# A decoder layer on one core: an earlier end of the output gate, key scaling in the own sum, scores in the key two, and the mix work of the last head spread out

## What is computed

```python
proj = rmsnorm(x) @ w_in                      # 4096 -> q, k, v, o, z of each head, and the rest
q, k = split(silu(causal_conv([m_q, m_k], w_conv)))
s = (q @ k.T) * exp(decay)                    # scores of one head, 256 x 256, causal
num, qn = s @ v, s.sum(-1)                    # "numerator" and its row sums
h = num / max(abs(qn), exp(-m))
h = rmsnorm(sigmoid(m_o) * h) * gain * silu(m_z)   # output gate o, gate z
out = rmsnorm(x + concat([h, attention * silu(a_z)]) @ w_out)
```

## Time and profile before

| | |
|---|---|
| median of 3 runs | 1752.15 us (1752.09 to 1752.25) |
| profiled execution, its own time | 1752.96 us |
| its span, first to last instruction | 1751.2 us |
| PE busy, matmuls | 1733.5 us, 8000 |
| DVE, ACT busy | 1313.6 us, 947.6 us |
| weight transfers (w_raw) | 614 of 512 KB, 202 GB/s over the span |
| heads' twos in the trace | 798 to 1401 us |

### The profile page before, as it was taken

The page is one execution under the profiler, slowest core; times in us unless marked ns, Lnnn a source line. Parts: engine busy times, 40 slices in busy tenths (PEclk is TensorE's granted clock), DMA queues, the critical chain, the costliest instruction groups (busy, mean ns, idle before and its releaser), DMA issues.

```text
span 1751.2 us, 23455 instructions
## 1 busy us (share of the span) xinstructions
PE 1733.5 (99%) x8000; PEld 1437.0 (82%) x8000; DVE 1313.6 (75%) x1679; ACT 947.6 (54%) x1318; POOL 20.0 (1%) x33
## 2 busy tenths in 40 slices
PE   9999999999999999999999999999999999999997
PEld 7888888888888888888888888888888788888886
DVE  7556786566675756668887888788878988888876
ACT  7535555455555555545555555555555665564553
POOL 0000000000000000000000000000000000000000
PEclk9999999999999999999999999999999999999999
DMA  9657656545455454555646564666565656666674
GB/s 383 241 179 234 214 195 221 185 157 183 154 188 170 158 182 161 174 181 204 216 169 217 205 215 169 217 206 212 174 213 208 206 187 212 216 217 215 217 262 182
DMA packets 98325, 354.59 MB, mean 202 GB/s; under 512 B 10688, under 2 KB 11200, under 8 KB 97472
## 3 DMA queue, kind: packets, MB, share of 16 engines
q1 hardware_dynamic: 94480, 336.96, 55.7%
q10 hardware_dynamic: 3760, 16.52, 2.7%
HBM read 347.67 MB, written 5.77 MB: 202 GB/s over the span
## 4 chain that ended last, share of the span: by engine, by line
PE 88%; DVE 5%; DMA 3%; issue 2%; ACT 1%; SPq 0%; DVEq 0%; POOLq 0%; ACTq 0%; POOL 0%
PE acc_a L721 12%; PE acc_a L723 12%; PE acc_a L722 12%; PE acc_b L721 11%; PE acc_b L723 11%; PE acc_b L722 11%; DMA w_raw<-in_w_all 3%; PE bank_xy L721 3%; PE bank_xy L722 3%; PE bank_xy L723 3%; PE bank_z L723 1%; PE bank_z L721 1%; PE bank_z L722 1%; PE bank_v L722 1%; PE bank_v L723 1%
## 5 line engine op out<-in xcount | busy, mean ns | idle before, releaser
L1775 DVE TENSOR_TENSOR w_split<-w_raw,w_split 128x1024 fp32r<-128x1024 f32 x495 | 599.5, 1222 | 263.0 <-ACT w_split L1253 254.3
L1253 ACT ACTIVATE w_split<-w_raw 128x1024 fp32r<-128x1024 f32 x494 | 518.1, 1056 | 366.1 <-PE acc_b L723 176.8
L721 PE MATMUL acc_a<-w_split,lhs_hi 128*128 128x512 f32 x968 | 379.9, 392 | 2.6 <-DVE stage L2087 2.4
L723 PE MATMUL acc_a<-w_split,lhs_lo 128*128 128x512 f32 x968 | 377.2, 390 | 0.0
L722 PE MATMUL acc_a<-w_split,lhs_hi 128*128 128x512 f32 x968 | 377.2, 390 | 0.0
L721 PE MATMUL acc_b<-w_split,lhs_hi 128*128 128x512 f32 x890 | 348.4, 391 | 0.0
L723 PE MATMUL acc_b<-w_split,lhs_lo 128*128 128x512 f32 x890 | 346.6, 389 | 0.0
L722 PE MATMUL acc_b<-w_split,lhs_hi 128*128 128x512 f32 x890 | 346.5, 389 | 0.0
L721 PEld LDWEIGHTS acc_a<-w_split,lhs_hi 128*128 128x128 f32 x968 | 181.8, 188 | 39.6 <-issue 2.5
L723 PEld LDWEIGHTS acc_a<-w_split,lhs_lo 128*128 128x128 f32 x968 | 181.7, 188 | 38.5
L722 PEld LDWEIGHTS acc_a<-w_split,lhs_hi 128*128 128x128 f32 x968 | 181.9, 188 | 33.8
(11 more groups left out here) (457 smaller groups left out, 2142.2 us busy)
## 6 DMA issues: line engine op xcount, KB each, us to landing
w_raw<-in_w_all SPq DMA_DIRECT2D x614, 512.0 KB
m_s_lo<-s_lo_kept ACTq DMA_DIRECT2D x4, 1536.0 KB, 7.5
wide<-in_x SPq DMA_DIRECT2D x8, 512.0 KB, 10.3
xres<-in_x ACTq DMA_DIRECT2D x8, 512.0 KB, 5.7
out_y<-wide SPq DMA_DIRECT2D x8, 512.0 KB, 3.6
gained_x<-in_x_cols_first SPq DMA_DIRECT2D x6, 512.0 KB, 7.5
toe<-in_toe_bias ACTq DMA_DIRECT2D x4, 512.0 KB, 5.0
gain_f<-in_final_norm_gain ACTq DMA_DIRECT2D x1, 2048.0 KB, 9.9
```

Of the source, the lines that this page charges most:

```text
L721: pe.matmul(dst, a[0], b[0], start=start, stop=False)
L723: return pe.matmul(dst, a[1], b[0], start=False, stop=stop)
L1253: act.activation(w_hi[:, cols], w_raw[:, cols], ACT.Copy).then_inc(hi_done, 1)
L1775: dve.tensor_tensor(w_lo[:, cols], w_raw[:, cols], w_hi[:, cols].bitcast(F32), ALU.subtract).then_inc(lo_done, 1)
```

## The change

- In a gate two the last four steps are now (14,0) (15,0) (14,1) (15,1) (`gates_in_turn`), in the stream of weights as well, and the own sums stand in slot 30.
- In a key two `key_scale` scales the sum of the shared parts in slot 19, once three of the four are done. VectorE's `scaled_own_sums` (slot 20) waits for that and adds the own banks, scaled in the same instruction. `conv_columns` is in front of step 21 and waits for the freed own banks; the pieces of the convolution move one slot up (`CONV_KEYS` 21).
- TensorE's scores stand in front of step 29 of the key two (step 9 of the plain block for head 0). sw follows in slot 29, its high part and the read of m_s_lo in slot 30, its low part in slot 31. The numerator stays in front of step 3 of the gate two.
- The eight parts of the mix in the last head stand in slots 10, 14, 18, 22, 26, 28, 31 and 31.

```diff
-MIX_TAIL, MIX_TURN = 24, 1
+MIX_TAIL, MIX_TURN = (10, 14, 18, 22, 26, 28, 31, 31), 1
+def gates_in_turn(order):
+
+    last = order[-2:]
+    return interleaved(order[:-2]) + tuple((c, h) for h in range(2) for c in last)
...
-SCORES, NUMERATOR = 0, 3
+NUMERATOR = 3
-CONV_V, CONV_KEYS = 1, 22
+CONV_V, CONV_KEYS = 1, 21
...
-                       interleaved(ORDER_M), (acc[0], acc[1]), [bx, by, bz, bv],
+                       gates_in_turn(ORDER_M), (acc[0], acc[1]), [bx, by, bz, bv],
...
-                    own_blocks(4 * h + B_MLSTM), True, head_pieces(h))
+                    own_blocks(4 * h + B_MLSTM), True, {NUMERATOR: [head_pieces(h)[1]]})
...
-                                                              (keys_scaled, h + 1)))]})
+                                                              (acc0_free, 4 * h + (B_MLSTM + 4)),
+                                                              (acc1_free, 4 * h + (B_MLSTM + 4))))],
+                     CONV_KEYS + 8: [head_pieces(h + 1)[0]]})
...
-            stream(B_MLSTM, 1, {CONV_V: [lambda: conv_columns(0, ((seven_free, 1),))]})
+            stream(B_MLSTM, 1, {CONV_V: [lambda: conv_columns(0, ((seven_free, 1),))],
+                                CONV_V + 8: [head_pieces(0)[0]]})
...
                 def key_scale():
-                    act.wait_ge(acc0_free, b + 4)
-                    act.wait_ge(acc1_free, b + 4)
+                    act.wait_ge(two_sums_done, keys_two(h).index * 3 + 3)
...
-                            (c + 6, qk_hi_part))
+                            (c + 6, qk_hi_part), (c + 9, sw_hi_part), (c + 9, input_sums_lo))
...
-                two_pieces = piece_map((0, values_hi), (SCORES, input_sums_lo), (SCORES + 1, sw_hi_part),
-                                       (SUMS_GATES, gate_product))
-                return two_pieces, conv_at, gates_at, (SUMS_KEYS, key_product), (CONV_KEYS - 1, key_scale)
+                two_pieces = piece_map((0, values_hi), (SUMS_GATES, gate_product))
+                return two_pieces, conv_at, gates_at, (SUMS_KEYS, key_product), (SUMS_KEYS + 1, key_scale)
...
+                def scaled_own_sums():
+                    w = keys_two(h)
+                    dve.wait_ge(keys_scaled, h + 1)
+                    dve.wait_ge(pe_used, w.start + (w.last(0) + 1))
+                    for t in range(TT):
+                        dve.scalar_tensor_tensor(m_shared[0][t], w.own[0][t][:, :], rstd[:, t:t + 1],
+                                                 m_shared[0][t], ALU.mult, ALU.add
+                                                 ).then_inc((acc0_free, acc1_free)[t], 1)
+
-                def sums_at(w, c, last):
+                def sums_at(w, c, own):
                     return (*[(c + part // 2, lambda part=part: shared_products(w, m_shared, part))
-                              for part in range(4)], (last, lambda: own_sums(w, 0)))
+                              for part in range(4)], (c + 2, own))
...
-                            (c + 5, qk_gate), (c + 7, qk_lo_part))
+                            (c + 5, qk_gate), (c + 7, qk_lo_part), (c + 8, scores),
+                            (c + 10, scores_lo))
...
-                two_pieces = ((SCORES, scores), (SCORES + 1, values_lo), (SCORES + 2, scores_lo),
+                two_pieces = ((1, values_lo),
...
-                              *sums_at(gates_two(h), SUMS_GATES, SUMS_GATES + 3))
+                              *sums_at(gates_two(h), SUMS_GATES, lambda: own_sums(gates_two(h), 0)))
...
-            gates(HEADS_M - 1, [(MIX_TAIL + c, lambda c=c: mix_lo(c)) for c in range(MIX_M)])
+            gates(HEADS_M - 1, [(MIX_TAIL[c], lambda c=c: mix_lo(c)) for c in range(MIX_M)])
```

More of the change, by code:

```diff
@@ L1150, in numerator @@
                     last.then_inc(num_ready, 1)
-                return {SCORES: [scores], NUMERATOR: [numerator]}
+                return scores, numerator
             def conv_columns(h, free):
@@ L1666, in input_sums_hi @@
                 act.activation(s_hi[:, f], s_raw[:, f], ACT.Copy).then_inc(s_hi_done, 1)
-            gates(HEADS_M - 1, {MIX_TAIL + c: [lambda c=c: mix_hi(c)] for c in range(MIX_M)})
+            gates(HEADS_M - 1, piece_map(*[(MIX_TAIL[c], lambda c=c: mix_hi(c)) for c in range(MIX_M)]))
             last_gates = piece_map(*head_pieces(HEADS_M - 1)[2](*GATES_LAST))
@@ L2320, in gates_at @@
                             (y, head_output))
-                two_pieces = ((SCORES, scores), (SCORES + 1, values_lo), (SCORES + 2, scores_lo),
+                two_pieces = ((1, values_lo),
                               (NUMERATOR + 1, lambda: normalise(0)),
                               (NUMERATOR + 1, lambda: normalise(1)),
-                              *sums_at(gates_two(h), SUMS_GATES, SUMS_GATES + 3))
-                return two_pieces, conv_at, gates_at, sums_at, own_sums
+                              *sums_at(gates_two(h), SUMS_GATES, lambda: own_sums(gates_two(h), 0)))
+                return two_pieces, conv_at, gates_at, sums_at, own_sums, scaled_own_sums
             def gates(h, late=(), behind=None):
@@ L2331, in keys @@
             def keys(h):
-                _, _, gates_at, sums_at, own_sums = head_pieces(h)
+                _, _, gates_at, sums_at, own_sums, scaled = head_pieces(h)
                 two_stream(keys_two(h), piece_map(
-                    *gates_at(*PRODUCTS_KEYS), *sums_at(keys_two(h), SUMS_KEYS, CONV_KEYS - 2),
+                    *gates_at(*PRODUCTS_KEYS), *sums_at(keys_two(h), SUMS_KEYS, scaled),
                     *head_pieces(h + 1)[1](CONV_KEYS)))
@@ L2635, in weight_stream @@
         gates = [block(w_in, run(col + h * BW)) for col in (C_MO, C_MZ)]
-        pairs += [gates[i][c] for c, i in interleaved(ORDER_M)]
+        pairs += [gates[i][c] for c, i in gates_in_turn(ORDER_M)]
         if h < HEADS_M - 1:
```

## The result

The changed kernel takes **1766.99 us** in the median of six runs (1764.26 to 1769.87), against 1752.2 for the kernel before: a ratio of 1.0085, with a 95% interval of 1.0074 to 1.0096. It is slower, as forecast, but by 14.8 us where 8.4 were forecast, and outside the range. Its runs spread over 5.6 us, those of the kernel before over 1.4.

What follows compares the result with a forecast made beforehand. TensorE, on 88% of the chain, was taken to bound the kernel. Gate twos -3.06, numerator -2.26, scores +4.5 and key scaling +9.2 sum to +8.4 us: 1760.5 us against the median of 1752.15, range 1754 to 1764.

Steps and rivals of the forecast that it cites:

- Key scaling, the holds: Before the key twos' transposes: scaling delays step 23's split, holds of 3.86, 3.07 and 3.96 us, +9.2 us.
- Rivals 1 and 2: Scaling fits before TensorE releases step 23: 1754.3 us, chance 0.10; helpers get a lead at new holds: 1747.9 us, chance 0.10.
- The clock: TensorE in the three long holds: the sum assumed full clock, going by the earlier trace, and added no loss.
- rival 3: Clock falls in the three long holds, products then 0.43 us apart: 4.8 us more, 1765.3 us, chance 0.05.
- Scores: In front of step 29, waiting for the low part of q and k: 1.13 us in four places, +4.5 us.
- Gate twos: At the gate twos' ends: own sums one step earlier, so the holds before the key product vanish, -3.06 us.
- What is late next there: After the gate twos' own sums: the output block's weights, said to be split before; no loss counted.
- Numerator: In the gate twos: waits only for the values' low part, -2.26 us, bounds -2.3 to -1.9.
- Nothing to spare: At the numerator: values' low part done at 970.5, TensorE asks at about 970.6; nothing left to wait.
- The mix parts: Last head's gate two: five low parts, 0.68 us each, run earlier and fit VectorE's idle time before quads.
- the moved read: The 1.5 MB read of s_lo, moved to slot 30 of the key two: takes 7.5 us, costs nothing.
- Rival 4: In the last gate two the moved mix parts find no cover, 5 x 0.68: 1763.9 us, chance 0.07.

Runs made afterwards that it cites:

- experiment 1: Changed kernel with twelve unread products on TensorE in the hold before the transposes of each key two: 1762.57 us, ratio 1.0059.
- experiment 6: Kernel before with only the gate twos' part, swapped last steps and own sums in slot 30: 1751.47 us, ratio 0.9995.
- experiment 7: Kernel before with only the mix parts of the last head spread over earlier slots: 1751.85 us, ratio 0.9999.
- experiment 3: Changed kernel with key scaling one slot later, in slot 20 behind the high part of step 23: 1757.64 us, ratio 1.0037.
- experiment 2: Kernel before with two extra unread copies on ScalarE ahead of key scaling in each key two: 1772.19 us, ratio 1.0112.
- experiment 8: Kernel of experiment 5 with the values' low part in slot 0 and the m_s_lo read back in slot 0 of gate twos: 1747.13 us, ratio 0.9970.
- experiments 4: Changed kernel with key scaling, its own sums and the transposes' place (in front of step 22) as before: 1756.98 us, ratio 1.0027.
- experiment 5: Changed kernel with transposes in front of step 22, key scaling in slot 20, scores in front of step 31: 1750.30 us, ratio 0.9991.

## Why the prediction was right or wrong

- **Key scaling, the holds: right.** The chain of rows gave 3.86, 3.07 and 3.96; at full clock they are 4.00, 3.01 and 3.79 (experiment 1), and ScalarE stands where it was said to, in front of the split of step 23. Rivals 1 and 2 are out: the transposes wait over 2.8 us.
- **The clock: the step that failed,** and the larger part of the miss: of the 6.5 us between the forecast of 1760.5 and the median, 4.4 go when TensorE is kept at work in the holds (experiment 1). The sum put the clock at nothing. I judged the three holds by the earlier trace rows, where 4.0 us after the last matmul still show 1.00, and gave rival 3 a chance of 0.05. In the holds the record falls 2.1 to 2.9 us after the last product's end (931.94 to about 934.8, 1113.63 to 1115.7, 1294.16 to 1296.6). One idle stretch that happened to keep the clock is no bound from below for others; the right reading was that 4.0 us had not been enough *there*. The prediction's own sign for rival 3, products 0.43 us apart, is there. The price of that rival, 1.6 us a hold from the warm-up, was too low in two of three: 2.7, 2.8 and 1.4 are lost, 7.0 for 4.8 in the profiled execution, because the clock comes back long after the work does. The Trainium skill (TensorE: Matmul & The Clock Gate, "Part 1: The HAM clock gate") says that the number of products at half clock at a kernel's start varies between runs of one kernel. Here the falls are in the kernel's middle; the mean clock of the changed kernel's six runs goes from 0.993 (1769.42 us) to 0.997 (1764.26), which agrees in kind.
- **Scores: right.** +1.10 each against 1.13. In the place shown the idle hold is 962.29 - 961.08 - 0.227 = 0.98, and the rest is lost in the restart.
- **Gate twos: right on the spot, wrong on the path.** They gain what was said, 0.6 a piece and 1.8 in the last head. "What is late next there" I named as the output block's weights, for the last head; for the others I didn't look, and the fours of the key two take back 1.9 us (experiment 6), a term that the sum put at nothing. The row that could have said so was in the list already: weights in a key two were the one small wait of the earlier trace rows.
- **Numerator: mis-sized by 0.4.** "Nothing to spare" was the right warning, and -1.88 is at the edge of the bounds (-2.3 to -1.9). VectorE's restart, which I took at 2.85 us from the earlier trace rows, is no constant: 3.27 in the changed kernel (there the profile names ScalarE's split as what it waited for), and 0.41 and 0.21 us of the wait remain in heads 1 and 2.
- **The mix parts: right; the moved read: open.** Rival 4 falls by experiment 7. TensorE waits for nothing of m_s_lo, but whether the read is worth nothing isn't shown: it may lengthen VectorE's restart. That is 2.85 and 1.77 us where the read is issued just behind the own sums, and 2.92 (experiment 3), 3.27, 4.36 and 4.83 where it is under way before, but these kernels differ in other things too.

## What to carry to other kernels

A hold of three microseconds on TensorE costs more than its length: price it with half of the work that follows at the lower clock, and don't take one idle stretch that kept the clock as leave for others. When a saved wait lies ahead of a stretch in which another engine is as slow as TensorE, follow the next steps until one of them has slack; if none has, the gain is gone. An operation that is folded into another one is only cheaper if its own wait doesn't stand in front of the splits that feed the main engine: here one slot made 9 us (1766.99 to 1757.64).

## What the runs showed of the hardware

- The granted clock fell in all six holds of 3 us and more that were traced with TensorE idle (changed kernel, experiment 2), 2.0 to 2.9 us after the last product, and came back 3.0 to 6.1 us after TensorE had begun to work again in the changed kernel. Each fall cost 1.4 to 2.8 us there, some 2.1 in experiment 2. After the kernel's last matmul 4.0 us passed at 1.00.
- The same holds with TensorE busy on products nobody reads cost no clock, so such products can be a cheap guard: 4.4 us of 14.8 came back.
- VectorE's first split after the end of the loop's body came after 1.8 to 4.8 us of "issue", in which the profile shows no wait (2.85 before, 1.77 in experiment 8, 4.36 in experiments 4 and 5, 4.83 in experiment 5).
